# Maps turned in banks 2 and 3 with one pair of score banks; late q/k tiles multiplied on GpSimd; the input norm's vector folded into the QKV weights; x turned as it lands

## The chip, the core and the metric

The kernel runs on one core of a Trainium2 chip. The metric is the device time of one launch, in microseconds (us). Before the change it is 1015.98 us, the median of three runs (1014.05 to 1016.07).

## What is computed

A trunk of two layers over 512 tokens of width 1024, all in float32. Layer 0 mixes tokens by differential attention (8 heads, two softmax maps each), layer 1 by a pooling mixer; both are followed by an MLP with a squared ReLU. The change touches layer 0's norm and attention:

```python
def rmsnorm(x, g):
    y = xf * lax.rsqrt(jnp.mean(xf * xf, axis=-1, keepdims=True) + EPS) * g
h = rmsnorm(x, norm_mix[0])
qkv = h @ w_qkv                                  # 1024 x 3072
q = partial_rope(rmsnorm(q, q_gain), cos, sin)   # 2 maps x 8 heads x 64
k = partial_rope(rmsnorm(k, k_gain), cos, sin)   # cos, sin from positions
s = q @ k.T * scale                              # per map, head, block of 128 queries
p = softmax(s)
a = p[0] - lam * p[1]
o = rmsnorm(a @ v, sub_gain) * (1 - lambda_init)
x = x + o @ w_o
...
x = x + square(relu(h @ w1)) @ w2                # each layer, h = rmsnorm(x, norm_mlp)
```

## The kernel before

Each engine has its own list of instructions, written out by hand in the order in which they run; semaphores tie the engines together. No scheduler moves anything. A float32 product on TensorE is three products in a reduced format: every operand is kept as a high part (a copy rounded to that format, made by ScalarE) and a low part (the rest, made by VectorE), and hi·hi, hi·lo and lo·hi are added up in PSUM. PSUM has eight banks of 128 x 512 float32: `pair[0]` is banks 0 and 1, `pair[1]` banks 2 and 3, and banks 4 to 7 are used one by one. In the rows, a name `pair` or `bank` is such a piece of PSUM, and `s_` stands before a tile in SBUF.

**Input part** (0 to about 136 us). x comes in four tiles of 128 tokens. VectorE multiplies each by the norm's vector, spread over all partitions (`g_bc`, L1127), TensorE turns the product `hn` eight 128x128 squares at a time into banks 4 to 7 (`turn_hn`, L1629), ScalarE keeps the high part (L856), VectorE the low part (L1133). The 1/rms of each token isn't needed for q and k, which are normed again, and is put onto v later. The QKV weights come in slabs of four pieces of 128 x 1024. A piece is split into its high part by ScalarE (one 1024-wide copy, `split_hi`) and its low part by VectorE (one 1024-wide subtraction, L1140, `split_lo`). Slabs 0 to 5 are QKV, 6 and 7 are w_o. The table `SPLIT` says in which attention steps the four pieces of the late slabs are split. Meanwhile GpSimd works out the angles of the rotary tables from the positions (`posi`, small elements brought by ScalarE's DMA queue; L595 to L647), ScalarE takes the sine, and GpSimd makes the tables. A finished q/k tile is copied by ScalarE into `qs`, squared by GpSimd (L676), summed by VectorE, rooted by GpSimd (L683, `qk_r`), multiplied by the root on VectorE (L1202) and rotated there (L1206 to L1209). There are 16 such tiles of 128 tokens by 4 heads (q or k); the first eight are finished before the attention steps begin.

**Attention part** (about 97 to 340 us). Step i handles one head and one block of 128 queries, 32 steps in all. On TensorE a step is, in this order: `scores(i)`, six products into the pair of banks i mod 2; the turn of the map of step i−2, four transposes into bank 4 (L1669); filler products (remaining QKV tiles, w_o, turns of x) in banks 6 and 7; in some steps a further turn of a q, k or o tile, also in bank 4 (a side turn below); `values(i−3)` into bank 5. All turns are counted in one sequence `TURNS`, and every turn waits for the low part of the turn before it in that sequence (`pe.wait_ge(turn_lo_done, k)`), since they share bank 4. Scores wait for the exponentials of two steps before:

```python
if i >= 2:
    pe.wait_ge(exp_done, 2 * (i - 1))
```

ScalarE in a step keeps the high part of the map turn, takes the two exponentials of the step (L937, each with a bias and a row sum), keeps the side turn's high part and a filler's copy, and makes a weight piece's high part where `SPLIT` says so. VectorE takes the maxima of the scores (L1260), mixes the two maps into one (L1287, into the tile `s_p_122` or `s_p_123` in turn), subtracts for the map's low part (L1224, `s_aT_lo`) and the side turn's (L1226, `s_qkT_lo` or `s_oT`), and does the q/k work and weight pieces above between them.

**After 340 us** come the MLP of layer 0 and layer 1; none of it is touched.

## Time and profile before

The profiled execution took 1017.12 us, of which its span, from the first to the last instruction on record, is 1015.3 us; TensorE's mean granted clock in it was 0.993 of full speed.

| engine | busy, us | share of the span |
|---|---|---|
| TensorE products (PE) | 981.1 | 97% |
| TensorE weight loads (PEld, beside PE) | 806.1 | |
| VectorE (DVE) | 855.7 | 84% |
| ScalarE (ACT) | 457.4 | 45% |
| GpSimd (POOL) | 346.7 | 34% |

The DMA engines moved 92.75 MB, 91 GB/s on average. A busy share is an average over stages with different limits, so it has to be read together with the same numbers by stretch of time. A full speed of 1.00 is TensorE at 2.4 GHz, 0.50 is its lower level of 1.2 GHz; a value between says how a stretch was shared between the two.

### The profile page before, as it was taken

What the parts mean: (1) busy time and instruction counts of PE and PEld (TensorE: products, weight loads), DVE (VectorE), ACT (ScalarE), POOL (GpSimd) and SP (SyncE); (2) the same over time, 40 slices, a digit from 0 to 9 for tenths busy, and PEclk for the clock granted to TensorE, in tenths of its full rate; (3) what the DMA queues carried; (4) which work ended last, traced back from release to release, by engine and by line L of the source; (5) the groups of instructions that cost most, each with busy time, mean ns of one, the idle gap of its engine ahead of it and who ended that gap; (6) DMA issues with size and microseconds to landing.
All of it is one profiled execution on the core that took longest, in us unless ns stands there. A gap on an engine that the chain in (4) does not pass through costs nothing.

```text
span 1015.3 us, 12819 instructions
## 1 busy us (share of the span) xinstructions
PE 981.1 (97%) x4724; PEld 806.1 (79%) x4724; DVE 855.7 (84%) x1107; ACT 457.4 (45%) x687; POOL 346.7 (34%) x307
## 2 busy tenths in 40 slices
PE   5999998989999899999999999999999999999998
PEld 5877776767788788888888888888888888888887
DVE  5595888987967999999998897687989999889883
ACT  5534544655644544534435343465353453443520
POOL 5860334211227175384841300350403404214000
PEclk9999999999999999999999999999999999999999
DMA  7432211220222333232323233302232323232202
GB/s 248 110 114 74 63 42 42 84 83 2 75 92 104 104 102 106 88 120 93 116 91 117 66 118 107 125 1 83 92 116 87 120 83 125 84 124 84 81 3 84
DMA packets 52046, 92.75 MB, mean 91 GB/s; under 512 B 8848, under 2 KB 9872, under 8 KB 51984
## 3 DMA queue, kind: packets, MB, share of 16 engines
q1 hardware_dynamic: 45888, 91.24, 27.0%
q10 hardware_dynamic: 6096, 0.69, 0.5%
q8 instruction: 38, 0.62, 0.3%
q14 instruction: 24, 0.20, 0.1%
HBM read 89.82 MB, written 2.10 MB: 91 GB/s over the span
## 4 chain that ended last, share of the span: by engine, by line
PE 79%; DVE 13%; issue 2%; POOL 2%; ACT 1%; DMA 1%; ACTq 0%; SPq 0%; DVEq 0%; POOLq 0%
PE bank L1611 39%; PE pair L1611 38%; DVE s_nmax L1260 2%; PE bank L1669 2%; DVE s_w_lo L1140 2%; DVE s_qkn L1202 1%; DVE s_aT_lo L1224 1%; DVE s_hT_lo L1345 1%; DVE s_p L1287 1%; DMA s_raw<-in_attn_w_qkv 1%; DVE s_qk_ss L1189 1%; DVE s_qkT_lo L1226 1%; DVE s_acc L1464 0%; DMA s_lbB<-in_mlp_w 0%; PE bank L1935 0%
## 5 line engine op out<-in xcount | busy, mean ns | idle before, releaser
L1140 DVE TENSOR_TENSOR s_w_lo<-s_raw,s_w_hi 128x1024 fp32r<-128x1024 f32 x96 | 160.1, 1685 | 14.2 <-ACT s_w_hi L816 7.7
L751 POOL TENSOR_TENSOR s_lt<-s_lbB,s_lbB 128x1024 f32<-128x1024 f32 x14 | 33.6, 2402 | 270.1 <-PE pair L1611 167.8
L1160 DVE TENSOR_TENSOR s_lbB_lo<-s_lbB,s_b_hi 128x1024 fp32r<-128x1024 f32 x64 | 119.1, 1884 | 0.0
L1611 PE MATMUL bank<-s_hT_hi,s_w_hi 128*128 128x512 f32 x256 | 100.5, 393 | 0.0
L846 ACT ACTIVATE s_b_hi<-s_lbB 128x1024 fp32r<-128x1024 f32 x64 | 67.2, 1053 | 73.7 <-POOL s_lbB L751 31.3
L1611 PE MATMUL pair<-s_hT_hi,s_w_hi 128*128 128x512 f32 x256 | 100.3, 392 | 0.0
L1611 PE MATMUL bank<-s_hT_hi,s_w_lo 128*128 128x512 f32 x256 | 99.7, 389 | 0.0
L1611 PE MATMUL pair<-s_hT_lo,s_w_hi 128*128 128x512 f32 x256 | 99.6, 389 | 0.0
L1611 PE MATMUL bank<-s_hT_lo,s_w_hi 128*128 128x512 f32 x256 | 99.6, 389 | 0.0
L1611 PE MATMUL pair<-s_hT_hi,s_w_lo 128*128 128x512 f32 x256 | 99.6, 389 | 0.0
L996 ACT ACTIVATE s_u_raw<-s_u_raw 128x512 f32<-128x512 f32 x64 | 40.4, 632 | 120.1 <-DVE s_u_raw L1363 120.1
L824 ACT ACTIVATE s_w_hi<-s_raw 128x1024 fp32r<-128x1024 f32 x60 | 61.7, 1052 | 54.0 <-PE pair L1611 25.3
L846 ACT ACTIVATE s_b_hi<-s_lt 128x1024 fp32r<-128x1024 f32 x42 | 44.4, 1058 | 65.8 <-POOL s_lt L751 56.5
L1399 DVE TENSOR_TENSOR s_acc<-s_acc,bank 128x512 f32<-128x512 f32 x84 | 55.5, 687 | 5.8 <-PE bank L1611 5.8
L1399 DVE TENSOR_TENSOR s_acc<-s_acc,pair 128x512 f32<-128x512 f32 x84 | 55.4, 686 | 4.8 <-PE pair L1611 4.7
L1611 PE MATMUL bank<-s_b_hi,s_u_hi 128*128 128x512 f32 x144 | 56.6, 393 | 1.9 <-DVE s_a_lo L1387 1.9
L1611 PE MATMUL pair<-s_b_hi,s_u_hi 128*128 128x512 f32 x144 | 56.6, 393 | 0.0
L1611 PEld LDWEIGHTS pair<-s_hT_lo,s_w_hi 128*128 128x128 f32 x256 | 48.1, 188 | 10.1 <-issue 0.2
L1611 PEld LDWEIGHTS bank<-s_hT_hi,s_w_lo 128*128 128x128 f32 x256 | 48.0, 188 | 10.1
L1611 PEld LDWEIGHTS bank<-s_hT_hi,s_w_hi 128*128 128x128 f32 x256 | 48.1, 188 | 10.0 <-issue 0.2
L1611 PEld LDWEIGHTS pair<-s_hT_hi,s_w_hi 128*128 128x128 f32 x256 | 48.1, 188 | 10.0 <-issue 0.2
L1611 PEld LDWEIGHTS pair<-s_hT_hi,s_w_lo 128*128 128x128 f32 x256 | 48.0, 188 | 10.0
(256 smaller groups left out, 2661.9 us busy)
## 6 DMA issues: line engine op xcount, KB each, us to landing
s_raw<-in_mlp_w SPq DMA_DIRECT2D x64, 512.0 KB, 3.6
s_lbB<-in_mlp_w SPq DMA_DIRECT2D x64, 512.0 KB, 3.2
s_raw<-in_attn_w_qkv SPq DMA_DIRECT2D x24, 512.0 KB, 3.6
s_raw<-in_attn_w_o SPq DMA_DIRECT2D x8, 512.0 KB, 3.2
s_x_nat<-in_x SPq DMA_DIRECT2D x4, 512.0 KB, 8.5
s_x_again<-in_x SPq DMA_DIRECT2D x4, 512.0 KB, 5.3
out<-s_acc SPq DMA_DIRECT2D x8, 256.0 KB, 2.0
s_raw<-in_pool_w SPq DMA_DIRECT2D x4, 256.0 KB, 2.6
```

The lines of the kernel that those rows point to most:

```text
L751: g.tensor_tensor(w2_raw[n][:], w2_raw[one][:], w2_raw[two][:], ALU.subtract).then_inc(t_done, 1)
L824: a.activation(w_hi[0][:, k * PIECE:(k + 1) * PIECE], raw[k][:], ACT.Copy).then_inc(w_hi_done, 1)
L846: a.activation(b_hi[home][:], w2_raw[n][:], ACT.Copy).then_inc(w2_hi_done, 1)
L996: a.activation(u_raw[:, f, :], u_raw[:, f, :], ACT.Square).then_inc(u_done, 1)
L1140: v.tensor_tensor(w_lo[slot][:, cols], raw[k][:], f32(w_hi[slot][:, cols]), ALU.subtract)\
L1160: v.tensor_tensor(w2_lo[n][:], w2_raw[n][:], f32(b_hi[home][:]), ALU.subtract).then_inc(w2_lo_done, 1)
L1189: link(v.tensor_reduce(qk_ss[:, n % 2, :], qsq[n % 2][:].rearrange("p (g d) -> p g d", d=QK), AX.X, ALU.add))
L1202: link(v.tensor_tensor(dst, qs[n % 4][:].rearrange("p (h m d) -> p h m d", h=4, m=2), r, ALU.mult))
L1260: v.tensor_reduce(nmax[:, i % 2, :], pair[i % 2][:], AX.X, ALU.max, negate=True).then_inc(max_done, 1)
L1399: last = v.tensor_tensor(dst, dst, src, ALU.add)
L1611: return nc.tensor.matmul(o, lhsT, rhs, start=start, stop=stop, **kw)
L1669: last = nc.tensor.transpose(bank[4][:, t * P:(t + 1) * P], src[t], ident[:])
```

## The change

- **Banks.** All scores go into banks 0 and 1. Maps are turned in banks 2 and 3 alternately, side turns alone in bank 4. Map turns and side turns are counted apart (`turned`, `turn_kept`, `turn_lo_done` for maps; `side_turned`, `side_kept`, `side_lo_done` for the others). A map turn waits for the low part of the map two before, a side turn for the side turn before. `scores(i)` waits for both exponentials of step i−1.
- **GpSimd multiplies late q/k tiles.** For tiles 8 to 15 the multiplication by the root moves from VectorE (L1202) to GpSimd, right behind the root; VectorE still does the rotation.
- **Norm vector into the weights.** `g_bc` and its multiplications go. The vector comes as `in_col`, one value per row of the weights: 1024 single elements, in the same queue ahead of the positions. For slabs 0 to 5 ScalarE's copy becomes two 512-wide copies with a scale, VectorE's subtraction two 512-wide scalar-tensor-tensor operations.
- **x turned as it lands.** TensorE transposes x itself, with 18 idle transposes of the identity ahead of the first tile and 16 ahead of the second. The products of the first slab are issued in another order, ScalarE's input squares stand behind the first slab's splits instead of between them.
- **SPLIT.** Slab 5 is split in steps 5 to 8 (was 6 to 9), slab 6 in 15, 16, 18, 19 (was 11 to 14).

The core of the diff:

```diff
-SPLIT = {4: (0, 1, 2, 3), 5: (6, 7, 8, 9), 6: (11, 12, 13, 14), 7: (27, 28, 29, 30), 8: (34, 34, 35, 35)}
+SPLIT = {4: (0, 1, 2, 3), 5: (5, 6, 7, 8), 6: (15, 16, 18, 19), 7: (27, 28, 29, 30), 8: (34, 34, 35, 35)}
...
+        def turn_bank(what, n):
+
+            return bank[2 + n % 2] if what == "map" else bank[4]
...
-                g.tensor_tensor(qk_r[:, n % 2, :], qk_v[:, n % 2, :], minus_half[:], ALU.pow)\
-                    .then_inc(qk_r_done, 1)
+                root = g.tensor_tensor(qk_r[:, n % 2, :], qk_v[:, n % 2, :], minus_half[:], ALU.pow)
+                if n >= 2 * NT:
+                    link(root)
+                    half, which, t = n // 8, n // 4 % 2, n % 4
+                    r = qk_r[:, n % 2, :].rearrange("p (h m) -> p h m", m=2).unsqueeze(3).to_broadcast([P, 4, 2, QK])
+                    dst = qkn[:, 4 * half:4 * half + 4, which, t, :].rearrange("p h (m d) -> p h m d", m=2)
+                    root = g.tensor_tensor(dst, qs[n % 4][:].rearrange("p (h m d) -> p h m d", h=4, m=2), r, ALU.mult)
+                root.then_inc(qk_r_done, 1)
...
-            act.dma_start(g_bc[:], norm_mix[0].partition_broadcast(P)).then_inc(small_loaded, 16)
-            with nc.allow_non_contiguous_dma("positions, 2 KB"):
+            with nc.allow_non_contiguous_dma("input gain as columns and positions, a few KB"):
+                act.dma_start(in_col[:], norm_mix[0].rearrange("(c p) -> p c", p=P)).then_inc(in_col_loaded, 16)
...
+                if s >= WO0:
+                    a.activation(w_hi[slot][:, k * PIECE:(k + 1) * PIECE], raw[k][:], ACT.Copy).then_inc(w_hi_done, 1)
+                    return
+                for c in range(2):
+                    cols = slice(c * BANK, (c + 1) * BANK)
+                    last = a.activation(w_hi[slot][:, k * PIECE + c * BANK:k * PIECE + (c + 1) * BANK], raw[k][:, cols],
+                                        ACT.Copy, scale=in_col[:, 2 * k + c:2 * k + c + 1])
...
                              bank[4 + n % 4][:].rearrange("p (c t) -> p c t", c=4), ACT.Copy)\
                     .then_inc(h_hi_done, 1)
 
-            input_squares(0)
             for t in range(NT):
-                split_hi(0, t, 0)
                 h_hi(2 * t)
                 h_hi(2 * t + 1)
-                if t + 1 < NT:
-                    input_squares(t + 1)
+                if t == 0:
+                    act.wait_ge(in_col_loaded, 16)
+                split_hi(0, t, 0)
+            for t in range(NT):
+                input_squares(t)
...
             def exps(i):
                 act.wait_ge(max_done, i + 1)
                 if i >= 2:
-                    act.wait_ge(turned, TURN_NO["map", i - 2] + 1)
+                    act.wait_ge(turned, i - 1)
                 for m in range(2):
-                    a.activation(probs[i % 2][:, m, :], bank[2 * (i % 2) + m][:], ACT.Exp,
+                    a.activation(probs[i % 2][:, m, :], bank[m][:], ACT.Exp,
                                  bias=nmax[:, i % 2, m:m + 1],
                                  accum_out=lsum[:, i, m:m + 1]).then_inc(exp_done, 1)
...
-            def input_gain(t):
-
-                dve.wait_ge(x_loaded[t], 16)
-                if t >= 2:
-                    dve.wait_ge(hn_turned, 2 * (t - 1))
-                v.tensor_tensor(hn[:, t % 2, :], x_nat[:, t, :], g_bc[:], ALU.mult).then_inc(hn_done, 1)
...
+                if s >= WO0:
+                    cols = slice(k * PIECE, (k + 1) * PIECE)
+                    v.tensor_tensor(w_lo[slot][:, cols], raw[k][:], f32(w_hi[slot][:, cols]), ALU.subtract)\
+                        .then_inc(w_lo_done, 1)
+                    return
+                for c in range(2):
+                    cols = slice(k * PIECE + c * BANK, k * PIECE + (c + 1) * BANK)
+                    last = v.scalar_tensor_tensor(w_lo[slot][:, cols], raw[k][:, c * BANK:(c + 1) * BANK],
+                                                  in_col[:, 2 * k + c:2 * k + c + 1], f32(w_hi[slot][:, cols]),
+                                                  ALU.mult, ALU.subtract)
+                last.then_inc(w_lo_done, 1)
...
-            input_gain(0)
+            dve.wait_ge(in_col_loaded, 16)
             for t in range(NT):
-                split_lo(0, t, 0)
-                if t + 1 < NT:
-                    input_gain(t + 1)
                 h_lo(2 * t)
                 h_lo(2 * t + 1)
+                split_lo(0, t, 0)
...
-                link(v.tensor_tensor(dst, qs[n % 4][:].rearrange("p (h m d) -> p h m d", h=4, m=2), r, ALU.mult))
+                if n < 2 * NT:
+                    link(v.tensor_tensor(dst, qs[n % 4][:].rearrange("p (h m d) -> p h m d", h=4, m=2), r, ALU.mult))
...
-            def turn_hn(t):
-                pe.wait_ge(hn_done, t + 1)
+            def turn_in(t):
+                pe.wait_ge(x_loaded[t], 16)
                 for half in range(2):
...
-                if k:
-                    pe.wait_ge(turn_lo_done, k)
-                else:
-                    pe.wait_ge(h_lo_done, 2 * NT)
+                if what == "map" and n >= MAP_BANKS:
+                    pe.wait_ge(turn_lo_done, n - MAP_BANKS + 1)
+                if what != "map":
+                    k = SIDE_NO[what, n]
+                    if k:
+                        pe.wait_ge(side_lo_done, k)
+                    else:
+                        pe.wait_ge(h_lo_done, 2 * NT)
                 for t in range(NT):
...
+                    last = nc.tensor.transpose(turn_bank(what, n)[:, t * P:(t + 1) * P], src[t], ident[:])
+                last.then_inc(turned if what == "map" else side_turned, 1)
+
+
+            def keep_turning(n):
+                for _ in range(n):
+                    nc.tensor.transpose(bank[0][:, 0:P], ident[:], ident[:])
+
+            keep_turning(18)
+            turn_in(0)
+            keep_turning(16)
+            turn_in(1)
+            for t, pieces in ((0, (0,)), (1, (0,)), (0, (1,)), (1, (1,)), (2, (0, 1)), (0, (2,)), (1, (2,)), (2, (2,)),
+                              (3, (0, 1, 2)), (0, (3,)), (1, (3,)), (2, (3,)), (3, (3,))):
                 project(t, bank[t], pieces)
-                if (t, pieces[-1]) in ((0, 0), (1, 1), (2, 2)):
-                    turn_hn(t + 1)
+                if (t, pieces) in ((1, (0,)), (1, (1,))):
+                    turn_in(2 + pieces[0])
...
-                    pe.wait_ge(turn_lo_done, TURN_NO["k", h] + 1)
-                if i >= 2:
-                    pe.wait_ge(exp_done, 2 * (i - 1))
+                    pe.wait_ge(side_lo_done, SIDE_NO["k", h] + 1)
+                if i >= 1:
+                    pe.wait_ge(exp_done, 2 * i)
                 cols = slice(t * P, (t + 1) * P)
                 for n, (lhs, rhs) in enumerate(((hi, hi), (hi, lo), (lo, hi))):
                     for m in range(2):
                         rows = slice(m * QK, (m + 1) * QK)
-                        last = mm(bank[2 * (i % 2) + m][:], lhs[rows, 0, cols], rhs[rows, 1, :], start=n == 0, stop=n == 2)
+                        last = mm(bank[m][:], lhs[rows, 0, cols], rhs[rows, 1, :], start=n == 0, stop=n == 2)
                 last.then_inc(scored, 1)
...
                 if i == STEPS + 1:
-                    pe.wait_ge(exp_done, 2 * (STEPS - 1))
+                    pe.wait_ge(exp_done, 2 * STEPS)
                     w_o_rest((0, 1), (0, 1))
                 if i == STEPS + 2:
-                    pe.wait_ge(exp_done, 2 * STEPS)
+                    pe.wait_ge(turn_lo_done, STEPS)
                     w_o_rest((2, 3), (0, 1))
                 if 2 <= i < STEPS + 2:
                     turn("map", i - 2)
```

Three places show what the change does to the order. The first is the start of TensorE's list, the turns of the input and the first products (`hn` is the multiplied input, `x_nat` the input itself, `w_hi`, `w_lo`, `hT_hi`, `hT_lo` the high and low parts of the first slab and the turned input). Before, then after:

```order
L1629 MATMUL bank<-s_ident,s_hn 128x128 [waits hn_done,consts]
L1629 MATMUL bank<-s_ident,s_hn 128x128 x7
L1611 MATMUL pair<-s_w_hi_53,s_hT_hi 128x512 [waits h_lo_done,w_lo_done]
L1611 MATMUL pair<-s_w_lo_55,s_hT_hi 128x512
L1611 MATMUL pair<-s_w_hi_53,s_hT_lo 128x512
L1611 MATMUL pair<-s_w_hi_53,s_hT_hi 128x512
L1611 MATMUL pair<-s_w_lo_55,s_hT_hi 128x512
L1611 MATMUL pair<-s_w_hi_53,s_hT_lo 128x512
L1629 MATMUL bank<-s_ident,s_hn 128x128 [waits hn_done]
L1629 MATMUL bank<-s_ident,s_hn 128x128 x7
```

```order
L1699 MATMUL pair<-s_ident 128x128 [waits consts]
L1699 MATMUL pair<-s_ident 128x128 x17
L1650 MATMUL bank<-s_ident,s_x_nat 128x128 [waits x_loaded0]
L1650 MATMUL bank<-s_ident,s_x_nat 128x128 x7
L1699 MATMUL pair<-s_ident 128x128 x16
L1650 MATMUL bank<-s_ident,s_x_nat 128x128 [waits x_loaded1]
L1650 MATMUL bank<-s_ident,s_x_nat 128x128 x7
L1632 MATMUL pair<-s_w_hi_53,s_hT_hi 128x512 [waits h_lo_done,w_lo_done]
L1632 MATMUL pair<-s_w_lo_55,s_hT_hi 128x512
L1632 MATMUL pair<-s_w_hi_53,s_hT_lo 128x512
```

Two tiles of x are now turned ahead of the first product, not one, and idle transposes stand before each; the turns wait for a DMA and no longer for VectorE.

The second is one attention step on TensorE: the end of `scores`, the map turn, the side turn behind the fillers, and the next step's scores (`s_p` a mixed map, `s_qkn` a rotated q/k tile, `s_qkT` its turned parts). Before, then after:

```order
L1611 MATMUL pair<-s_qkT_hi_58,s_qkT_lo_59 128x512 x2
L1669 MATMUL bank<-s_ident,s_p_123 128x128 [waits turn_lo_done,a_done]
L1669 MATMUL bank<-s_ident,s_p_123 128x128 x3
L1611 MATMUL bank<-s_w_hi_53,s_hT_hi 128x512 [waits qk_copied]
...
L1669 MATMUL bank<-s_ident,s_qkn 128x128 [waits turn_lo_done,qk_ready]
L1669 MATMUL bank<-s_ident,s_qkn 128x128 x3
L1611 MATMUL bank<-s_val_85,s_aT_hi 128x256 [waits o_kept,turn_lo_done]
...
L1611 MATMUL pair<-s_qkT_hi_58 128x512 [waits exp_done]
...
L1669 MATMUL bank<-s_ident,s_p_122 128x128 [waits turn_lo_done,a_done]
```

```order
L1632 MATMUL pair<-s_qkT_hi_58,s_qkT_lo_59 128x512 x2
L1693 MATMUL pair<-s_ident,s_p_123 128x128 [waits turn_lo_done,a_done]
L1693 MATMUL pair<-s_ident,s_p_123 128x128 x3
L1632 MATMUL bank<-s_w_hi_53,s_hT_hi 128x512 [waits qk_copied]
...
L1693 MATMUL bank<-s_ident,s_qkn 128x128 [waits side_lo_done,qk_ready]
L1693 MATMUL bank<-s_ident,s_qkn 128x128 x3
L1632 MATMUL bank<-s_val_85,s_aT_hi 128x256 [waits o_kept,turn_lo_done]
...
L1632 MATMUL pair<-s_qkT_hi_58 128x512 [waits exp_done]
...
L1693 MATMUL pair<-s_ident,s_p_122 128x128 [waits turn_lo_done,a_done]
```

Nothing moved in the row order. The map turn goes into a pair bank, where it was in the bank of the side turns, and the side turn waits on its own semaphore. The wait `exp_done` of the scores has another count, two exponentials more, which the rows do not print.

The third is VectorE in its steps 11 and 12, about 170 to 180 us: the mixing of a map, a weight piece, the next q/k tile (`s_w_lo` the low part of a piece, `s_qs` and `s_qk_r` the copied tile and its root, `s_rt` halves of the rotation). Before, then after:

```order
L1287 SCALAR_TENSOR_TENSOR s_p_123<-s_p_123,s_mixc 128x512 [waits mix_known]
L1189 TENSOR_REDUCE s_qk_ss<-s_qsq_139 128x8 [waits qk_r_done,qk_squared]
L1190 TENSOR_SCALAR s_qk_v<-s_qk_ss 128x8 [waits dve_chain]
L1140 TENSOR_TENSOR s_w_lo_55<-s_raw_49,s_w_hi_53 128x1024 [waits w_hi_done]
L1226 SCALAR_TENSOR_TENSOR s_oT_66<-bank,s_sub_col,s_oT_66 128x512 [waits turn_kept]
...
L1287 SCALAR_TENSOR_TENSOR s_p_122<-s_p_122,s_mixc 128x512 [waits mix_known]
L1202 TENSOR_TENSOR s_qkn<-s_qs_137,s_qk_r 128x4x128 [waits qk_r_done]
L1206 TENSOR_TENSOR s_rt_140<-s_qkn,s_rope_ck 128x128 [waits dve_chain]
L1207 TENSOR_TENSOR s_rt_141<-s_qkn,s_rope_sk 128x128 [waits dve_chain]
...
L1140 TENSOR_TENSOR s_w_lo_55<-s_raw_50,s_w_hi_53 128x1024 [waits w_hi_done]
L1226 SCALAR_TENSOR_TENSOR s_qkT_lo_59<-bank,s_qk_col,s_qkT_hi_58 128x512 [waits turn_kept]
```

```order
L1308 SCALAR_TENSOR_TENSOR s_p_123<-s_p_123,s_mixc 128x512 [waits mix_known]
L1208 TENSOR_REDUCE s_qk_ss<-s_qsq_137 128x8 [waits qk_r_done,qk_squared]
L1209 TENSOR_SCALAR s_qk_v<-s_qk_ss 128x8 [waits dve_chain]
L1247 SCALAR_TENSOR_TENSOR s_oT_66<-bank,s_sub_col,s_oT_66 128x512 [waits side_kept]
...
L1308 SCALAR_TENSOR_TENSOR s_p_122<-s_p_122,s_mixc 128x512 [waits mix_known]
L1226 TENSOR_TENSOR s_rt_138<-s_qkn,s_rope_ck 128x128 [waits qk_r_done]
L1227 TENSOR_TENSOR s_rt_139<-s_qkn,s_rope_sk 128x128 [waits dve_chain]
...
L1247 SCALAR_TENSOR_TENSOR s_qkT_lo_59<-bank,s_qk_col,s_qkT_hi_58 128x512 [waits side_kept]
```

The multiplication by the root and both weight pieces are gone from these steps. The multiplication is on GpSimd; the pieces are of slab 6, now split four to five steps later. The next maxima and the map's low part, left out here, stand between in both kernels.

## Rows read from the trace of the kernel before

**Rows 1.** Busy us by stretch: PE, PEld, DVE, ACT, POOL; PEclk, DMA share, GB/s.

```profile
39.00:66.00 27.00, 26.21 (x117) 21.39 (x115) 23.79 (x54) 10.37 (x14) 24.66 (x18) 1.00 0.48 125
...
136.00:173.00 37.00, 31.72 (x165) 24.98 (x166) 30.80 (x59) 15.28 (x30) 17.49 (x12) 0.91 0.16 57
...
173.00:200.00 27.00, 25.91 (x156) 20.53 (x153) 25.69 (x45) 16.41 (x33) 6.55 (x4) 1.00 0.22 78
...
200.00:280.00 80.00, 73.03 (x467) 56.02 (x466) 66.73 (x122) 46.65 (x99) 13.79 (x12) 1.00 0.16 53
```

**Rows 2.** Who waited for whom, TensorE, 96 to 280: total, times, longest.

```profile
PE bank L1669 <- DVE s_qkT_lo L1226: 6.6, 6, 1.9
...
PE bank L1669 <- DVE s_aT_lo L1224: 4.7, 7, 1.8
```

**Rows 3.** Timeline, steps 10 and 11: start, length, engine, line, operation, idle before.

```profile
156.46 0.63 PE L1669 MATMUL bank<-s_ident,s_p 128*128 128x128 f32 x4 [1.61 <-DVE s_qkT_lo L1226]
...
161.65 0.40 PE L1611 MATMUL pair<-s_qkT_hi,s_qkT_lo 64*128 64x512 f32 x2
...
164.37 1.21 DVE L1260 TENSOR_REDUCE s_nmax<-pair 128x2 f32<-128x1024 f32 x1
```

**Rows 4.** Busy time by stretch, TensorE alone, after the stop at 163.94: granted clock.

```profile
164.00:167.00 3.00, 3.00 (x10) 0.52 0.48 175
```

**Rows 5.** Timeline, steps 17, 18 and 19, 20: exponentials' end, maxima, next scores.

```profile
205.70 0.20 ACT L937 ACTIVATION_READ_ACCUMULATOR s_p<-pair,s_nmax 128x1 f32 x1
...
206.81 0.51 PE L1611 MATMUL pair<-s_qkT_hi 64*128 64x512 f32 x2
...
213.30 1.21 DVE L1260 TENSOR_REDUCE s_nmax<-pair 128x2 f32<-128x1024 f32 x1
...
214.49 0.50 PE L1611 MATMUL pair<-s_qkT_hi 64*128 64x512 f32 x2
...
215.79 0.20 ACT L937 ACTIVATION_READ_ACCUMULATOR s_p<-pair,s_nmax 128x1 f32 x1
```

**Rows 6.** DMA queues in 6:7, 7:8 and 8:9 (two rows): packets, MB, share.

```profile
q10 hardware_dynamic: 157, 0.00, 8.8%
...
q10 hardware_dynamic: 98, 0.00, 5.4%
...
q1 hardware_dynamic: 129, 0.34, 90.6%
...
q10 hardware_dynamic: 131, 0.00, 7.3%
```

**Rows 7.** Timeline of the input part: GpSimd, ScalarE, then TensorE.

```profile
10.62 0.77 POOL L612 CAST s_posf<-s_posi 128x4 f32<-128x4 int32 x1 [8.62 <-DMA s_posi<-in_positions]
...
30.61 0.24 POOL L647 TENSOR_SCALAR s_ropet<-s_ropet 128x64 f32<-128x64 f32 x1
...
33.90 0.26 ACT L901 ACTIVATE s_ropet<-s_ropet 128x64 f32<-128x64 f32 x1
...
34.06 3.89 ACT L816 ACTIVATE s_w_hi<-s_raw 128x1024 fp32r<-128x1024 f32 x4
...
37.86 2.41 ACT L880 ACTIVATE s_qs<-pair,s_in_r 128x512 f32<-128x512 f32 x4
...
65.93 0.50 PE L1611 MATMUL pair<-s_w_hi,s_hT_hi 128*128 128x512 f32 x1 [0.79 <-DVE s_w_lo L1140]
```

**Rows 8.** Single lines of code: count, duration ns min/median/max, first and last start.

```profile
L606 POOL TENSOR_SCALAR s_ropet<-s_ropet x9: 287/369/1325, 12.5 to 29.7; 128x32 f32<-128x32 f32 x7, 128x64 f32<-128x64 f32 x2
...
L705 POOL TENSOR_TENSOR s_oc<-s_oc,s_o_r x8: 1040/1076/1543, 138.2 to 293.6; 128x512 f32<-128x512 f32 x8
...
L1202 DVE TENSOR_TENSOR s_qkn<-s_qs,s_qk_r x16: 678/684/1560, 44.3 to 181.9; 128x512 f32<-128x512 f32 x16
...
L1287 DVE SCALAR_TENSOR_TENSOR s_p<-s_p,s_mixc x32: 735/744/934, 93.8 to 277.8; 128x512 f32<-128x512 f32 x32
...
L1140 DVE TENSOR_TENSOR s_w_lo<-s_raw,s_w_hi x96: 1209/1220/3448, 9.0 to 966.5; 128x1024 fp32r<-128x1024 f32 x96
```

77 lines of the change are left out of this document (36 added, 41 removed).

## The prediction

> **What bounds the kernel now.** I read the busy shares first, then the same by stretch, then what TensorE waited for, then the timeline at those waits. TensorE is busy 97% of the span, so a gain can come only from its idle time, from stretches at the lower of its two clock levels, or from less TensorE work; the change removes no products. By stretch, the idle time lies in the attention part: 5.3 us (37.00 − 31.72) in 136 to 173, where the granted clock is also 0.91, then 1.1 us in 173 to 200 and 7.0 us in 200 to 280 [rows 1]. The waits say what it is: 6.6 us in six waits and 4.7 us in seven, all at L1669, a turn (four transposes into bank 4) waiting for VectorE to take the low part of the turn before it [rows 2]. The reader is to see in one of them that the probabilities s_p are ready and yet TensorE stands 1.61 us until s_qkT_lo is done, since both use bank 4 [rows 3]. After such waits the clock fell to its lower level, 1.2 GHz: 0.52 on average over 164 to 167 [rows 4].
>
> The input part is another matter: from 12.1 to 65 us TensorE runs with hardly a gap, and stops at 65.93 for the last weight piece of the third slab [rows 7]. What it waits for there is VectorE, which works off the q/k tiles after GpSimd's rope tables.
>
> **Map turns out of bank 4.** All 13 waits of [rows 2] are a map turn behind a side turn or the reverse. With maps in banks 2 and 3 a map turn waits for the low part of the map two before it, and side turns for each other; those are four steps apart or more, or one step with a whole step of work between. So 6.6 + 4.7 = 11.3 us of waits lose their cause: 1.3 us before 136, 5.3 in 136 to 173, 1.1 in 173 to 200, 3.6 after. The clock loss of the worst stretch goes with them: 37.0 × 0.09 = 3.3 us [rows 1], since no idle time of 1.6 us or more is left there. Together 14.6 us, the upper end.
>
> What is late next? In 136 to 173 VectorE is busy 30.8 us, and TensorE without the idle time and at full clock would need 31.7 − 3.3 = 28.4 [rows 1]. VectorE would then bound, but the change unloads it just there. Three to four q/k multiplications go to GpSimd, at 0.68 us, and up to 1.56 where GpSimd was in the way [rows 8]: about −3.5. One weight piece is split a step sooner, outside the stretch, −1.2 to −2.0. Against that come dearer pieces (+0.5, below) and VectorE held up by the new GpSimd work (+1.0, below). That is about 27.3 us, just under TensorE's 28.4. Two engines so evenly loaded in a chain of waits lose something to each other: I take 1.0 us. In 173 to 200 two or more pieces of 1.22 us leave VectorE for its steps 15 to 19, and it has room after 200 (66.7 of 80 us busy) [rows 1]. The term is −(14.6 − 1.0) = −13.6; its lower end, with VectorE as the bound at 30.8 us in that stretch and nothing else changed, is 14.6 − (30.8 − 28.4) = 12.2, or some 8 if the late steps give back their 3.6 too.
>
> **One score pair.** scores(i) now waits for both exponentials of i−1, not i−2. Queued behind it on TensorE are that step's map turn, its filler products and values. The start of the scores against the end of the exponentials one step before, over the 31 steps: in 27 the scores already began later, as at 206.81 after an end at 205.90, where the last accumulator read ends [rows 5]. In four they began sooner: by 1.50 us at 214.49 (the end is at 215.99), by 0.48, by 0.47 and by 0.06 (the first of them in [rows 5]). That sums to 2.5 us. At 214.49 part of it is absorbed, as TensorE afterwards waited 1.5 us in all for s_p and s_oc; but steps with 0.03 to 0.6 us of slack become late when TensorE runs faster, and a piece now stands in VectorE's steps 18 and 19, ahead of the maxima of steps 20 and 21. I take +3.0 (1.0 to 8). The chain in one step is 0.97 of scores, 1.23 of maxima, 1.5 of exponentials and small handovers: 3.8 us, against a mean step of 6.0, so it fits where VectorE is prompt.
>
> **GpSimd's multiplications.** Eight instructions of 128x512 leave VectorE (0.68 us each) and cost GpSimd about 1.08 each [rows 8], which is idle there half the time or more [rows 1]. They go in behind the root and are read a step later, some 5 us, so nobody waits. But the engines hold each other up: L606 takes 0.29 us at best and up to 1.32 where VectorE works on two SBUF tiles, and the q/k multiplication 1.56 instead of 0.68 [rows 8]. Per tile VectorE gains between 0.68 − 1.08 = −0.4 and 1.56. I take +0.4, already in the 27.3 above. The Trainium skill, "GPSIMD Engine Reference", section "1. Specifications", speaks against this edit: the SBUF interfaces are shared with VectorE, with contention from its instructions that have two SBUF inputs. By that rule, the two durations of L606 agree. Were all 8 × 1.08 us of it to block VectorE, the edit would lose 8 × 0.4 = 3.2 us of VectorE time rather than gain, which is the third rival.
>
> **The input part.** The multiplications by g_bc (L1127) go, and TensorE turns x as it lands, warmed by 34 idle transposes. I cost this at nothing gained: TensorE's early finish of the first slab is hidden behind the chain that follows. That chain gets a new head. The gain now arrives as in_col, 1024 elements of 4 bytes instead of rows, and the positions (512 elements) queue behind it. While the large loads run, the small packets pass about one for one with the large ones: 131 against 129 in one us [rows 6]. From about 3 us, 1024 / 131 = 7.8 us puts in_col at 11, and 512 / 131 = 3.9 puts the positions at 15 instead of 10.6 [rows 6, 7]. Bounds: 98 to 157 packets per us in the neighbouring slices [rows 6] put the positions at 12.8 to 18.7; no delay gives 10.6.
>
> So the first weight piece is scaled at 11 to 12.4 us and its low part is ready at 14; products begin at 14, not 12.1, with TensorE idle for 4 us before, so probably at the low clock again. 96 products and two turns later it is at 38 to 40. GpSimd's angle chain took 10.62 to 30.85 = 20.2 us, of which five operations stretched by VectorE to over 1 us, as L606 at its longest, made up 4.4 [rows 7, 8]. Now only three pieces fall into it: 20.2 − 1.8 = 18.4 us, ending at 33.4. The sine ran at 33.90, held by ScalarE's own DMA issues and table load, which now come sooner; so it runs at 33.5 to 34. The four pieces then take 8 × 0.60 (from four 512-wide scaled copies in 2.41 us) = 4.8 instead of 3.89, and the first copied tile comes at 39.2 instead of 38.5 [rows 7]. Products of the second slab need it, and began at 39 to 39.6 (114 products before 65.14, at 26.21 / 117 = 0.224 us [rows 1, 7]). So +0.3. VectorE pays for each piece two instructions of 0.744 (those of L1287, also scalar-tensor-tensor and 512 wide), less some overlap, instead of one of 1.22 [rows 8]: +0.15 to +0.27, four pieces before the stop at 65.93, +0.7. Front in all: +1.0, with bounds −1 (the chain itself starts no sooner) and +5 (positions at 18.7).
>
> The Trainium skill, "DMA: Bandwidth & Descriptors", section "Queues, rings and completion order", says a DMA engine drains a packet of typically 9 to 17 descriptors from one ring before it switches. By that rule small elements would pass in groups, in_col and the positions would both be there by about 6 us, and the front would be worth −1, not +1. The counts of [rows 6] do not show it: the small elements are packets of their own.
>
> **After 280 us** nothing is changed; VectorE and the weight loads follow TensorE, so what is gained stays.
>
> **Sum.** −13.6 + 3.0 + 1.0 = −9.6 us. The profiled execution took 1017.12 us (span 1015.3) and would take 1007.5; the median is 1015.98, 1.1 less, so the forecast is 1006.4, say 1006.5. A difference within 0.2% (2.0 us) can't be told from none.
>
> **Rivals.** (1) The input chain is not delayed, by small elements in groups, and the engines don't hamper each other: −14.6 + 1.5 − 1 = −14.1, 1002. For it: VectorE loses the most work where TensorE waits most. Against it: the packet counts.
> (2) The positions land at 18 or later: front +4 to +5, 1010.
> (3) VectorE becomes the bound of the attention part: GpSimd's work blocks it in full (+3.2), and the saving in 136 to 173 is 6.2 instead of 7.6; with late steps giving back half their 3.6, −9.6 + 3.2 + 1.4 + 1.8 leaves −3.2, 1013. For it: VectorE is at 95% in 173 to 200 [rows 1]. Against: it loses two or more pieces there.
> (4) The slower side: the waits only change place. TensorE gets to scores(i) sooner and stands there until the exponentials of i−1, because VectorE takes the maxima late; the idle stretches and the low clock stay. Its place is the score pair, its price the 2.5 us above with nothing of the 14.6 recovered, and the front: 1016 + 2.5 + 1.0 = 1019.5. It decides if VectorE's delay before the maxima is over about 1.9 us in most steps (step 5.7 less the chain of 3.8). For it: the maxima at 164.37 began 2.3 us after the scores' end at 162.05 [rows 3], and in three of 32 steps it was over 2 us. Against: in 18 it was below 0.5 (last scores row and next maxima row of each step).
>
> **How the numbers follow.** Forecast and its own range, 1003 to 1010.5: 0.58. Rival 1: 0.08. Rival 2: 0.07. Rival 3: 0.09. Rival 4: 0.10. The rest, 0.08, lies between: 0.07 within 0.2%, 0.01 slower. Of rival 3, 0.02 fall within 0.2%. So faster 0.80, same 0.09, slower 0.11. The range 1001 to 1014 holds the first four.
>
> **What would show it.** Right: no wait of map turns on s_qkT_lo or s_aT_lo of the other kind; granted clock near 1.00 from 136 to 173; a new wait of the pair on ScalarE's s_p, 2 to 4 us in all; GpSimd's first conversion at about 15 us; the stop for the third slab's last piece near 67. Wrong: waits at the pair above 8 us, clock still at 0.9 in the middle, or the second slab starting later than 42 us.

## The result, and the profile after

The changed kernel takes 1002.76 us, the median of four runs (1001.83 to 1003.70), against 1015.11 before (four runs, 1014.05 to 1016.07): a ratio of 0.9871, 95% interval 0.9847 to 0.9895. The forecast was 1006.5, with 1003 to 1010.5 as its own range and 1001 to 1014 as the whole one: the time lies just below the former and inside the latter. The profiled execution took 1001.83 us, span 1000.0, mean clock 0.993.

Busy time by stretch after, with the columns of [rows 1]:

```profile
39.00:66.00 27.00, 23.49 (x102) 18.79 (x101) 25.78 (x57) 9.71 (x16) 20.61 (x13) 1.00 0.35 74
136.00:173.00 37.00, 37.00 (x218) 29.62 (x218) 33.97 (x72) 18.77 (x41) 17.66 (x14) 1.00 0.14 43
173.00:200.00 27.00, 26.26 (x164) 21.23 (x164) 23.21 (x41) 17.65 (x36) 3.74 (x4) 1.00 0.12 40
200.00:280.00 80.00, 75.88 (x463) 60.09 (x462) 67.17 (x117) 44.67 (x91) 18.08 (x15) 0.98 0.23 72
```

TensorE is without a gap from 136 to 173 at full clock, where it had lost 5.3 us to waits and ran at 0.91. The gap is now in 39 to 66, where it was 0.8 us and is 3.5.

What TensorE waited for after, 0 to 280 us (the answer to [rows 2]):

```profile
PE pair L1632 <- ACT s_p L958: 3.6, 4, 1.6
PE pair L1632 <- DVE s_w_lo L1160: 3.5, 2, 2.2
PE pair L1699 <- POOL s_ident L585: 1.8, 1, 1.8
PE bank L1650 <- DMA s_x_nat<-in_x: 1.0, 1, 1.0
PE bank L1632 <- DVE s_oc L1289: 1.0, 2, 0.7
```

Not one turn of a map, q, k or o waits for a low part any more: all 13 waits are gone. New are 3.6 us of scores waiting for exponentials (the one pair) and 2.7 us more for weight pieces (3.5, where it was 0.8). The longest of the former, steps 19 and 20, as forecast (the answer to [rows 5]):

```profile
199.26 1.21 DVE L1281 TENSOR_REDUCE s_nmax<-pair 128x2 f32<-128x1024 f32 x1
...
202.09 0.50 PE L1632 MATMUL pair<-s_qkT_hi 64*128 64x512 f32 x2 [1.57 <-ACT s_p L958]
```

The starts of the scores divide the 15.3 us that the span lost: the first scores begin at 82.25 us (84.81 before), the last at 254.06 (269.06). So the front gave 2.6 us, the attention steps 12.4, and what comes behind them 0.3. The gain between the medians is 12.35 us, since before's profiled execution (1017.12) was 2.0 us above its median and this one is 0.9 below.

The input part after, first GpSimd, ScalarE and TensorE, then VectorE's third and fourth piece of the third slab and the products that wait for them (the answer to [rows 7]):

```profile
9.94 0.19 POOL L617 CAST s_posf<-s_posi 128x4 f32<-128x4 int32 x1 [7.94 <-DMA s_posi<-in_positions]
...
27.36 0.24 POOL L652 TENSOR_SCALAR s_ropet<-s_ropet 128x64 f32<-128x64 f32 x1
...
27.63 0.26 ACT L922 ACTIVATE s_ropet<-s_ropet 128x64 f32<-128x64 f32 x1 [2.91 <-POOL s_ropet L652]
...
9.82 0.48 PE L1632 MATMUL pair<-s_w_hi,s_hT_hi 128*128 128x512 f32 x1
...
57.22 2.19 DVE L1160 SCALAR_TENSOR_TENSOR s_w_lo<-s_raw,s_in_col,s_w_hi 128x512 fp32r<-128x512 f32 x2
...
59.47 0.50 PE L1632 MATMUL pair<-s_w_hi,s_hT_hi 128*128 128x512 f32 x1 [1.28 <-DVE s_w_lo L1160]
...
61.90 1.41 DVE L1160 SCALAR_TENSOR_TENSOR s_w_lo<-s_raw,s_in_col,s_w_hi 128x512 fp32r<-128x512 f32 x2
...
63.36 0.49 PE L1632 MATMUL pair<-s_w_hi,s_hT_hi 128*128 128x512 f32 x1 [2.23 <-DVE s_w_lo L1160]
```

The positions are in use at 9.94, not at 15, and the sine runs at 27.63 (33.90 before), released by GpSimd and no longer held by ScalarE's own list. The piece that the third slab waits for is there at 63.3, against 65.9 before: the 6.3 us won at the sine have shrunk to 2.6, most of it because three of the four pieces took 2.19 us instead of 1.22.

### The profile page after: what moved, and what is told of

The parts are those of the page before. It is cut to its first block, busy times and chain, and to the rows that moved or that the text cites. A ratio compares the mean times of both kernels' runs of the same rounds, so it can differ in the third digit from the quotient of the medians.

```text
span 1000.0 us, 12928 instructions
## 1 busy us (share of the span) xinstructions
PE 981.4 (98%) x4758; PEld 808.9 (81%) x4758; DVE 853.4 (85%) x1119; ACT 462.7 (46%) x711; POOL 350.8 (35%) x315
## 4 chain that ended last, share of the span: by engine, by line
PE 84%; DVE 8%; POOL 3%; issue 2%; DMA 1%; ACT 1%; ACTq 0%; SPq 0%; POOLq 0%; DVEq 0%
PE bank L1632 43%; PE pair L1632 38%; PE pair L1693 1%; DVE s_w_lo L1160 1%; PE bank L1693 1%; DMA s_posi<-in_positions 1%; DVE s_hT_lo L1366 1%; DVE s_nmax L1281 1%; DVE s_w_lo L1155 1%; DVE s_acc L1485 0%; DVE s_qkn L1222 0%; DMA s_lbB<-in_mlp_w 0%; DVE s_qk_ss L1208 0%; PE bank L1966 0%; DVE s_xT L1588 0%
## 5 line engine op out<-in xcount | busy, mean ns | idle before, releaser
L1155 DVE TENSOR_TENSOR s_w_lo<-s_raw,s_w_hi 128x1024 fp32r<-128x1024 f32 x72 | 125.7, 1766 | 6.3 <-ACT s_w_hi L842 6.3
L1182 DVE TENSOR_TENSOR s_lbB_lo<-s_lbB,s_b_hi 128x1024 fp32r<-128x1024 f32 x64 | 123.3, 1950 | 0.0
L1632 PEld LDWEIGHTS bank<-s_hT_lo,s_w_hi 128*128 128x128 f32 x256 | 48.1, 188 | 10.0 <-issue 0.2
```

The source lines that it names most:

```text
L1155: v.tensor_tensor(w_lo[slot][:, cols], raw[k][:], f32(w_hi[slot][:, cols]), ALU.subtract)\
L1182: v.tensor_tensor(w2_lo[n][:], w2_raw[n][:], f32(b_hi[home][:]), ALU.subtract).then_inc(w2_lo_done, 1)
L1632: return nc.tensor.matmul(o, lhsT, rhs, start=start, stop=stop, **kw)
```

## The experiments

Differences in traces are told by the start of the first and the last scores; each kernel was also timed in five rounds beside the kernel before. Most executions of the kernel before took either 1013 to 1014 or 1016 to 1019 us, so the median beside a run is anything from 1013.8 to 1016.3, and the ratios, which follow the means more than the medians, carry some of that too. "Clock loss" is the length of a stretch times what its granted clock lacks to 1.00, added up over pieces of 2 us.

**Banks alone.** The kernel before with the bank and semaphore edits, all else as it was:

```diff
-                    last = nc.tensor.transpose(bank[4][:, t * P:(t + 1) * P], src[t], ident[:])
+                    last = nc.tensor.transpose(turn_bank(what, n)[:, t * P:(t + 1) * P], src[t], ident[:])
...
-                if i >= 2:
-                    pe.wait_ge(exp_done, 2 * (i - 1))
+                if i >= 1:
+                    pe.wait_ge(exp_done, 2 * i)
```

> The kernel before with the banks alone: scores in banks 0 and 1, maps turned in banks 2 and 3, side turns in bank 4, each kind with its own count. Input part, q/k multiplications and SPLIT as before. Theory A (the shared bank 4 is the cause): the waits of map turns on s_qkT_lo and of side turns on s_aT_lo go, the granted clock in 136 to 173 is near 1.00, and nearly all of the attention part's gain (12.4 us between the first and the last scores) is there: 9 to 12 us less than before. Rival B (VectorE was the second bound, 30.8 us busy in a stretch where TensorE needs 28.4): without the unloading of VectorE new waits on s_p, s_qkn or s_w_lo appear in 136 to 173, and no more than 5 to 8 us are won. My own sum of the prediction, 11.3 + 3.3 less 2.4 for VectorE as the bound there and less 3.0 for the score pair, gives 9.2.

1007.77 us against 1013.79 (ratio 0.9929, 0.9910 to 0.9948). From the first to the last scores 8.0 us less than before, and 4.5 less gained than by the whole change. Waits of TensorE in the attention part, then two of them in the timeline:

```profile
PE pair L1619 <- ACT s_p L944: 3.6, 4, 1.6
PE bank L1619 <- DVE s_val L1221: 2.0, 1, 2.0
PE bank L1619 <- DVE s_oc L1276: 1.9, 2, 1.2
```

```profile
159.42 0.36 PE L1619 MATMUL bank<-s_val,s_aT_hi 128*128 128x256 f32 x1 [1.16 <-DVE s_oc L1276]
...
177.99 0.50 PE L1619 MATMUL bank<-s_w_hi,s_hT_hi 128*128 128x512 f32 x1 [2.02 <-DVE s_val L1221]
```

VectorE is nearly full in 136 to 173 here (columns of [rows 1]):

```profile
136.00:173.00 37.00, 35.84 (x203) 28.41 (x202) 36.36 (x70) 19.54 (x39) 18.09 (x12) 1.00 0.22 72
```

Theory A holds for the cause: the turn waits are gone and the granted clock is 1.00. Its size, 9 to 12 us, does not: 6.0 us between the medians, 7.2 by the ratio and 8.0 in the trace are rival B's 5 to 8, and so are the full VectorE and the two new waits, though these are on s_oc and s_val and not on the tiles that it had named.

**Input part alone.** The kernel before with `in_col`, the scaled pieces and x turned as it lands.

> The kernel before with the input part alone: norm vector as columns in the QKV weights, x turned as it lands behind idle transposes, squares behind the splits. Theory A (the input part is worth what the first scores show, 84.81 to 82.25 us): 2 to 3 us less than before, first scores at about 82.3. Rival B (the prediction's term: +1.0, because small elements are late): 1 us more. Rival C (in the attention part the dearer pieces cost VectorE, which is loaded there in the old banks): the first scores come 2.6 sooner, but half of that or more is lost by 280 us.

1015.24 us against 1013.79 (ratio 0.9997, 0.9980 to 1.0015): nothing that can be told. In its trace the last stop ends at 63.84 us, 0.5 behind the changed kernel, but the first scores begin only at 84.32: after that stop of 2.23 us the granted clock fell (0.76 in 62 to 66, 0.81 in 66 to 70), where the changed kernel's trace has 1.00 in both. It is the execution and not the old banks: the trace of the run "SPLIT as before", whose list is the changed kernel's up to there, has the same fall (0.82 and 0.75) and first scores at 84.21. Of the twelve executions the four fastest took 1011.6 to 1012.0 us, 1.6 under the fastest of the kernel before, so the gain is there in some and not in others. Rival C is not borne out: the attention steps were 1.0 us shorter, not longer.

**Multiplications back on VectorE.** The changed kernel with

```diff
-                if n < 2 * NT:
-                    link(v.tensor_tensor(dst, qs[n % 4][:].rearrange("p (h m d) -> p h m d", h=4, m=2), r, ALU.mult))
+                link(v.tensor_tensor(dst, qs[n % 4][:].rearrange("p (h m d) -> p h m d", h=4, m=2), r, ALU.mult))
```

and without GpSimd's.

> The changed kernel with the late q/k tiles multiplied on VectorE again (L1222), nothing on GpSimd. Theory A (the multiplications on GpSimd are worth 8 x 0.68 us of VectorE, but VectorE is not the bound at most steps): 0.5 to 2.5 us more than the changed kernel, as waits on s_qkn or s_p between 125 and 190. Rival B (they contend with VectorE for SBUF, so that VectorE wins nothing): within 0.5 us of the changed kernel, or faster.

1003.20 us (ratio 0.9881, 0.9861 to 0.9902): the changed kernel's time within the measurement, rival B's in size. Its reason, that VectorE wins nothing by GpSimd's multiplications, is not borne out: VectorE is busy 36.03 us in 136 to 173 here and 33.97 in the changed kernel. The trace has one further wait of the pair, 0.78 us ahead of the scores at 153.16. From the first to the last scores it is 2.0 us longer than the changed kernel's, of which 1.7 is clock loss behind a stop that both have.

**SPLIT as before.**

```diff
-SPLIT = {4: (0, 1, 2, 3), 5: (5, 6, 7, 8), 6: (15, 16, 18, 19), 7: (27, 28, 29, 30), 8: (34, 34, 35, 35)}
+SPLIT = {4: (0, 1, 2, 3), 5: (6, 7, 8, 9), 6: (11, 12, 13, 14), 7: (27, 28, 29, 30), 8: (34, 34, 35, 35)}
```

> The changed kernel with the steps of SPLIT as before: slab 5 in steps 6 to 9, slab 6 in 11 to 14. Theory A (VectorE has about 1 us to spare per step once the banks are apart): slab 5 one step later stands ahead of products that need it, 0 to 2 us more. Rival B (SPLIT makes no difference): within 0.5 us. Rival C (slab 6 in steps 15 to 19 is what delays the maxima of steps 19 and 20 by putting pieces ahead of them): the waits of the scores on s_p, 3.6 us in the changed kernel, fall to 2 or less, and it is 1 us faster.

1003.77 us (0.9884, 0.9862 to 0.9906), again not to be told from the changed kernel. One wait of 0.70 us on s_val at 175.4 is new, so if theory A holds at all, it is at the lower end of its 0 to 2 us; the waits on s_p are 3.5 us, so rival C is out.

**One score pair alone.** The kernel before with

```diff
-                if i >= 2:
-                    pe.wait_ge(exp_done, 2 * (i - 1))
+                if i >= 1:
+                    pe.wait_ge(exp_done, 2 * i)
...
-                        last = mm(bank[2 * (i % 2) + m][:], lhs[rows, 0, cols], rhs[rows, 1, :], start=n == 0, stop=n == 2)
+                        last = mm(bank[m][:], lhs[rows, 0, cols], rhs[rows, 1, :], start=n == 0, stop=n == 2)
```

and the same bank for exponentials and maxima.

> The kernel before with one score pair alone: all scores in banks 0 and 1, each waiting for both exponentials of the step before; maps still turned in bank 4 with the side turns. It measures the price of the pair by itself. Theory A (the four steps with negative slack are delayed by their 2.5 us, and a little follows): 2 to 4 us more than before, shown as waits on s_p between 210 and 275. Rival B (TensorE makes it up, since it waits for s_p and s_oc later in the same steps anyway): within 1 us of before. Rival C (the waits come in most steps): 6 us or more.

1016.30 us against 1016.21 (ratio 1.0008, 0.9994 to 1.0022), in time rival B. Its waits, 96 to 280:

```profile
PE bank L1669 <- DVE s_qkT_lo L1226: 6.5, 6, 1.9
PE bank L1669 <- DVE s_aT_lo L1224: 4.7, 7, 1.8
PE pair L1611 <- ACT s_p L937: 2.6, 3, 1.6
PE bank L1611 <- DVE s_oc L1268: 0.6, 1, 0.6
PE bank L1669 <- POOL s_oc L705: 0.2, 1, 0.2
```

The pair costs waits of 2.6 us, of which 0.8 comes off s_oc of L705 (1.0 before). From the first to the last scores the trace is 0.3 us longer, but some 1.5 us of clock loss that before's trace had in step 8 are absent, so the price is about 1.8. It is not only the waiting: behind the longest of the new waits, 1.56 us ahead of the scores at 213.57, the granted clock fell to 0.79 over 211 to 219, a loss of 1.7 us, where before's trace has 1.00.

**No idle transposes.**

```diff
-            keep_turning(18)
             turn_in(0)
-            keep_turning(16)
             turn_in(1)
```

> The changed kernel without the 34 idle transposes at the start. Theory A (they keep TensorE's products at 0.23 us apart from the first one on, but the end of the first slab is hidden behind GpSimd's angle chain and VectorE's pieces): the first 12 to 20 products stand 0.43 us apart, the first slab ends later, and from the second slab on the times are the same: within 0.5 us. Rival B (the clock's loss is carried through): 2 to 3 us more.

1000.92 us (1000.27 to 1001.28; ratio 0.9860, 0.9842 to 0.9878): about 2 us less than the changed kernel, which neither theory had. The first five products are slow, fewer than expected (0.43 us apart, though the profile gives a granted clock of 1.00 there), and yet the third slab's last piece is ready 0.7 us sooner. VectorE and GpSimd here, then GpSimd in the changed kernel:

```profile
57.14 1.41 DVE L1160 SCALAR_TENSOR_TENSOR s_w_lo<-s_raw,s_in_col,s_w_hi 128x512 fp32r<-128x512 f32 x2
...
57.94 1.51 POOL L681 TENSOR_TENSOR s_qsq<-s_qs 128x512 f32<-128x512 f32 x1 [0.39 <-ACT s_qs L899]
```

```profile
57.60 1.27 POOL L681 TENSOR_TENSOR s_qsq<-s_qs 128x512 f32<-128x512 f32 x1
```

In the changed kernel GpSimd's squares started 0.38 us into the piece (57.22 to 59.41), which took 2.19 us. Here TensorE's lag makes the copied tile late, the squares start 0.80 us into it, and the piece takes 1.41. A collision costs VectorE 0.78 us. That two short instructions leave a gap which the other engine enters is my reading of these rows, not a run's result. TensorE's total stop falls from 3.5 to 1.4 us, and the first scores begin at 81.50, 0.75 us sooner.

**Late positions.** The changed kernel with 2048 single elements more in the queue ahead of the positions:

```diff
                 act.dma_start(in_col[:], norm_mix[0].rearrange("(c p) -> p c", p=P)).then_inc(in_col_loaded, 16)
+                for k, vec in enumerate((norm_mix[1], norm_mlp[0])):
+                    act.dma_start(extra[:, k, :], vec.rearrange("(c p) -> p c", p=P)).then_inc(extra_loaded, 16)
```

> The changed kernel with 2048 further single elements (two more vectors as columns, never read) loaded between the gain and the positions, in the same queue. It makes the case that the prediction took: late positions. Theory A (the angle chain is the head of the front, so what is lost there is lost at the first scores): with the 700 elements per us of the first microsecond the positions land 3 us later, with the 100 to 160 per us of later ones over 10 us later; GpSimd's first conversion moves with them, and the first scores by the same time less at most 1 us. Rival B (the products and VectorE's pieces are the bound): the first scores move by less than a third of it.

1007.60 us (ratio 0.9931, 0.9914 to 0.9948). GpSimd's first conversion is at 16.01 (6.1 us later), the first scores at 87.22 (5.0 later), as theory A says. The run delays more than it was meant to: ScalarE was held until 9.93 by issuing the DMAs, so the products began at 15.03, 5.2 us later than in the changed kernel, and lost another 3.4 us of clock by 22 us. What speaks for the positions is the wait that ends last there, on VectorE's piece, at the end of a list that moved with the sine (33.22, 5.6 later):

```profile
68.30 0.50 PE L1636 MATMUL pair<-s_w_hi,s_hT_hi 128*128 128x512 f32 x1 [1.10 <-DVE s_w_lo L1164]
```

But TensorE's only other stop is the one at 15.03, so with the positions in time its own lateness would still have cost up to 3.9 of the 5.0 us, all but this stop. The run does not part the two. The queues' packets, first two rows the changed kernel in 3:4, then this kernel in 11:12 and in 14:15 (q1 the large loads, q10 the small elements):

```profile
q1 hardware_dynamic: 64, 0.20, 50.9%
q10 hardware_dynamic: 698, 0.00, 38.4%
```

```profile
q1 hardware_dynamic: 164, 0.37, 103.3%
q10 hardware_dynamic: 164, 0.00, 11.0%
...
q1 hardware_dynamic: 112, 0.20, 55.9%
q10 hardware_dynamic: 877, 0.00, 50.6%
```

Where the large loads take 95% of the engines or more, small packets pass one for one with them, to within three packets in each of the six slices from 8 to 14 us. Where they take 51 and 56%, 698 and 877 small ones pass; at 68 to 80%, in the changed kernel's 4 to 7 us, it is 163 to 342.

**Pieces sooner.** The changed kernel with the third slab's low parts earlier in VectorE's list:

```diff
+SOONER = {3: (0,), 4: (1, 2), 5: (3,)}
...
-                    if s:
+                    if n in SOONER:
+                        for k in SOONER[n]:
+                            split_lo(2, k, 0)
+                    if s > 1:
                         split_lo(s + 1, t, (s + 1) % 2)
```

> The changed kernel with the third slab's low parts sooner in VectorE's list: piece 0 ahead of the sum of q/k tile 3, pieces 1 and 2 ahead of tile 4, piece 3 ahead of tile 5 (was 4, 5, 6, 7). Theory A (TensorE's two stops at 58 and 61 us, 1.28 and 2.22 us, are only this order; the q/k tiles that come later have room until their turns at about 75): both stops go or fall under 0.5 us, the first scores come 2.5 to 3.5 us sooner, and it beats the changed kernel by about 3 us. Rival B (VectorE is full, 25.8 of 27 us, so the wait moves to the turns of q and k, or to the fourth slab's pieces): under 1 us is won.

999.32 us (997.80 to 999.65; ratio 0.9842, 0.9823 to 0.9860): 3.4 us under the changed kernel. TensorE has no gap in this stretch:

```profile
39.00:66.00 27.00, 27.00 (x121) 22.37 (x120) 25.46 (x54) 10.68 (x17) 20.62 (x14) 1.00 0.37 81
```

VectorE does the same work there (25.46 us busy, 25.78 in the changed kernel); only its order was wrong. The first scores begin at 79.46.

**The changed kernel again**, beside the three that follow.

> The changed kernel once more, unedited, so that it stands beside the kernels of this group on one chip and has more runs. Theory A (its time is 1002.8 us with a spread of one or two clock falls of 1 to 2 us each): median 1001.5 to 1003.5. Rival B (the version without idle transposes is really faster, not only measured elsewhere): the median here is 1 us or more above the 1000.9 us of that one.

1002.99 us (1001.75 to 1003.63), ratio 0.9863 (0.9846 to 0.9879). All eight executions of the changed kernel (1001.75 to 1003.70) lie above all four without idle transposes, as rival B says. But those ran on another chip, and the ratios, 0.9863 and 0.9860, can't be told apart; the traces show 0.75 to 1.1 us at the first scores. So about 1 us is shown, and the rest of the 2 is not.

**Both edits together.**

> The changed kernel with both edits: the third slab's low parts sooner and no idle transposes. Theory A (with the stops gone, TensorE's products bound the front, so that the slow ones at the start are paid): 1.5 to 2.5 us more than with the sooner pieces alone (999.3 us). Rival B (the other gain adds: a start that is later keeps GpSimd's squares away from VectorE's pieces, 0.78 us each): 1 us less.

999.79 us (998.90 to 1001.89; 0.9830, 0.9814 to 0.9845). The trace has theory A's loss, first scores 1.3 us later than with the sooner pieces alone; in the times the two can't be told apart.

**Input part as before**, banks, GpSimd and SPLIT changed.

> The changed kernel with the input part as before: rows of the norm vector multiplied into x on VectorE, x turned behind it, weight pieces 1024 wide. Banks, GpSimd's multiplications and SPLIT as changed. Theory A (the input part is worth the 2.6 us of the first scores): 2 to 3 us more than the changed kernel, nothing more in the attention steps. Rival B (1024-wide pieces of 1.22 us in place of two of 1.41 give VectorE room in steps 0 to 8): 1 us or less. Rival C (the other way round, the whole difference between banks alone and the changed kernel, 5 us, is the input part): 4 us or more.

1004.57 us (1002.77 to 1004.99), 1.6 above the changed kernel beside it. First scores at 84.96, 2.3 to 2.7 later than in the two traces of the changed kernel, and nothing more up to the last scores (171.9 us, against 171.8 and 172.7): theory A, though the times show a little less than it said.

**Sooner pieces, multiplications on VectorE.**

> The kernel with the sooner pieces, but the late q/k tiles multiplied on VectorE. Theory A (the multiplications on GpSimd save waits of about 0.8 to 1.1 us in the steps where VectorE is full, 136 to 180 us): 0.5 to 1.5 us more than with the sooner pieces alone. Rival B (GpSimd's work holds VectorE up as much as it saves): the same or less.

999.53 us (ratio 0.9830, 0.9815 to 0.9846), the same as with them on GpSimd. The trace has a wait of 0.81 us at 149.1 that they save (its attention steps are 2.0 us longer than with the sooner pieces alone, 1.7 of it clock loss); the times don't resolve it.

## Why the prediction was right, and where it was wrong

In the main the mechanism was the forecast one, and the number is good in part by luck. Between the traces the sum missed by 5.7 us (9.6 forecast, 15.3 measured: 1.8 in the attention steps, 3.6 in the front, 0.3 behind), between the medians only by 2.9, since before's profiled execution lay further above its median than I had reckoned and the changed kernel's lay below. Of the five signs that I had named for "right", three came (the waits of the turns, the clock, the waits of the pair), and the two of the input part, positions at 15 and the stop near 67, did not.

**Map turns out of bank 4** (−13.6): right in kind and nearly in size. All 13 waits went and the clock of 136 to 173 rose from 0.91 to 1.00. With the pair, the attention steps gave 12.4 us where −13.6 + 3.0 = −10.6 was forecast. The claim that VectorE would bound there but for its unloading is shown: banks alone left VectorE busy 36.36 of 37 us and waits of 3.2 us on s_val and s_oc at 158 and 176. Undoing the GpSimd multiplications costs 0.2 us of median, the SPLIT 0.8, each less than the measurement tells. Undoing both costs 3 to 5 (banks alone against the version with the old input part: 3.2 between the medians, 5.4 by the ratios 0.9929 and 0.9876, each known to 0.2%; 4.4 between their traces from first to last scores, 1.7 of it clock loss). They cover the same shortage, and either is nearly enough. I had added them up.

**Clock** (−3.3): true of the execution I read, not of all. Of 43 further executions of the kernel before, 16 ran at a mean clock of 0.997 and took 1013.2 to 1014.0 us; the other 27, at 0.990 to 0.995, took 1014.4 to 1019.4. And the clock was not simply won: the loss in 136 to 173 went, but the changed kernel loses 1.7 us anew at 202 to 206, behind the pair's longest stop, and 1.7 at 318 to 322. The mean clock is 0.993 in both profiled executions. In the second trace of the changed kernel the loss behind that stop is 3.4 us.

**One score pair** (+3.0, 1.0 to 8): waits of 3.6 us in four steps, the four I had named; alone 1.8 in the trace. The sum had no clock loss in this term. Of the twelve traces with one pair eleven have one, of 1.7 or 3.4 us, behind the stop of 1.56 or 1.57 us ahead of step 20's scores, so the pair cost more than its waits; it stayed inside the range.

**GpSimd's multiplications** (+0.4 per tile won): never resolved in a time, though each of the two traces without them has a further wait of 0.8 us. The Trainium skill's rule on the shared interface ("GPSIMD Engine Reference", section "1. Specifications") was weighed against the wrong edit: the trace agrees with it at the scaled weight pieces, which also have two SBUF inputs: 2.19 us where GpSimd's squares start in the first half, 1.41 where they don't.

**The input part** (+1.0, measured −2.6) is the step that failed: "From about 3 us, 1024 / 131 = 7.8 us puts in_col at 11, and 512 / 131 = 3.9 puts the positions at 15". I took the count of a slice in which the large loads fill the engines for one in which they are only starting. In 3 to 5 us 1040 small packets passed; the gain was in use at 6.8 and the positions at 9.94. From there my chain held: 17.7 us of GpSimd (18.4 forecast), then the sine. The run with late positions made the case I had assumed, with products as late as the positions, and cost the first scores 5.0 us. The second term was wrong the other way: four pieces were to cost 0.7 us and cost 3.1: four times 0.19 by the two-instruction form, as forecast, and three times 0.78 by the collision with GpSimd's squares, which was not in the sum. The sine came 5.9 to 6.4 us sooner than forecast, the pieces cost 2.4 more; that leaves about the 3.6 between +1.0 and −2.6. The −2.6 is one pair of traces. In the four with the old input part the first scores begin between 83.80 and 84.96, in the three of the new one with these stops and without a clock fall there between 82.25 and 82.64, so the gain lies between 1.2 and 2.7 us; in two more traces the fall took most of it. "TensorE warmed by idle transposes, at nothing gained" was right for the gain; they cost about 1 us in the traces and up to 2 in the times, by timing alone.

Of the rivals, the first gave 1002, close to the time: its undelayed positions came true, its engines that don't hamper each other did not. Its page's rule, packets of 9 to 17 descriptors ("DMA: Bandwidth & Descriptors" of the Trainium skill, section "Queues, rings and completion order"), isn't what the counts show: one for one in the full stretch. The slower side never came near: only four scores waited, and the idle time did not come back.

## What to carry to other kernels

Before a resource shared by two chains is split, ask what the next bound has to spare: the banks gave 8 of the attention part's 12.4 us, most of the rest came only with a lighter VectorE, by whichever edit. Where an engine is nearly full, the order of its list decides which engine stands: moving four weight pieces forward, at no cost, won more than the whole input part. A rate of small DMA elements has to be read from a slice with the same load beside it.

## What the runs showed of the hardware

- Small DMA elements pass one for one with the packets of large loads that fill the engines (164 and 164, 169 and 169 in a slice of 1 us); in the changed kernel's 7 to 9 us, with fewer than 100 left to pass, it was 59 beside 136 and 30 beside 188. Beside loads that took 51 and 56% of the engines it was 698 and 877 per us.
- A 128x1024 subtraction on VectorE stays at 1.22 us [rows 8] where GpSimd's squares start beside it (before, at 53.18 and 57.01 us, and it is the squares that take 1.74 instead of 1.04); cut into two scaled halves it takes 1.41, and 2.19 when the squares start in the first half.
- TensorE's clock after a stop is not settled by the stop: after the same stop of 1.57 us at the same scores the granted clock of 204 to 208 us was 0.75 in one execution of the changed kernel and 0.50 in the other:

```profile
204.00:208.00 4.00, 4.00 (x22) 0.75 0.44 131
```

```profile
204.00:208.00 4.00, 4.00 (x15) 0.50 0.45 131
```

(TensorE alone). The clock loss behind this stop was 1.7 us in the first and 3.4 in the second, and none in the trace with both edits together, whose stop was 1.56 us. One trace overstates or understates a change by as much.
